# Feature products of a hybrid attention and delta-rule step: eight together in every second step, or four in each

## What is computed

```python
h = _rms(x, w_norm)
proj = h @ w_in                                  # 1024 -> 6152 columns
aq, ak, av, az, bq, bk, bv, bz, bb, ba, ga, gb = jnp.split(proj, ...)
# attention: 4 heads, each a difference of two softmaxes over 64 features
p = softmax(mask(q k^T / 8));  p = p[:, :, 0] - lam * p[:, :, 1];  o_a = rms(p @ v) * silu(az)
# delta rule: short convolution of bq, bk, bv, then chunks with a 128 x 128 state a head
s = s * gl + kg^T (u - w s);  o_b = rms(qg s + qk v_new) * silu(bz)
y = sigmoid(ga) * (o_a @ w_up_a) + sigmoid(gb) * (o_b @ w_up_b);  out = x + y @ w_out
```

## Time and profile before

| | |
|---|---|
| three runs | 1506.8, 1513.76, 1515.07 us (median 1513.76) |
| profiled execution | 1516.26 us |
| its span, first to last instruction | 1514.5 us |
| mean granted clock of TensorE | 0.946 |
| PE busy | 1332.6 us (88%) |
| DVE, ACT, POOL busy | 695.8, 277.7, 453.5 us |
| joint stretch | about 231 to 1237 us |

### The profile page before, as it was taken

How to read it: one execution, slowest core, us unless ns; L and a number is a source line. 1 busy time by engine, 2 the same in 40 slices (tenths; PEclk the granted TensorE clock), 3 DMA queues, 4 the chain that set the end, 5 groups by cost and what they waited for, 6 DMA issues and landing times.

```text
span 1514.5 us, 20691 instructions
## 1 busy us (share of the span) xinstructions
PE 1332.6 (88%) x7189; PEld 684.1 (45%) x7189; DVE 695.8 (46%) x1151; ACT 277.7 (18%) x556; POOL 453.5 (30%) x358
## 2 busy tenths in 40 slices
PE   3999999996997996998887888489999978999999
PEld 3444344453453443444444444145555533554443
DVE  4446205658576665775545454834442204343001
ACT  3112103323222322331111211011211110111000
POOL 0122203425333333443555554346461000000000
PEclk9899999998999997998999999689999999889999
DMA  8120407564655566375798789468786264253121
GB/s 259 27 93 29 148 0 242 176 207 138 205 174 190 167 194 194 118 225 177 215 308 293 246 290 342 160 182 283 281 299 225 78 215 144 84 189 117 55 84 57
DMA packets 167181, 269.25 MB, mean 178 GB/s; under 512 B 29618, under 2 KB 66297, under 8 KB 165916
## 3 DMA queue, kind: packets, MB, share of 16 engines
q1 hardware_dynamic: 107636, 149.64, 31.0%
q10 hardware_dynamic: 59440, 118.28, 23.3%
HBM read 221.63 MB, written 46.40 MB: 177 GB/s over the span
## 4 chain that ended last, share of the span: by engine, by line
PE 69%; DVE 12%; ACTq 4%; issue 4%; DMA 4%; ACT 4%; SPq 2%; POOL 0%; DVEq 0%; POOLq 0%
PE ps L1627 24%; PE ps L1574 11%; PE ps L1940 7%; PE ps L1917 5%; PE ps L1677 4%; PE ps L1650 3%; ACTq L875 2%; ACTq L878 2%; PE ps L1716 2%; DVE sc L1206 1%; SPq L602 1%; DMA work<-in_cache_v 1%; DVE qkv L1382 1%; PE ps L1745 1%; PE ps L1748 1%
## 5 line engine op out<-in xcount | busy, mean ns | idle before, releaser
L1627 PE MATMUL ps<-hT,wbuf 128*128 128x512 f32 x1152 | 546.1, 620 | 0.0
L1627 PEld LDWEIGHTS ps<-hT,wbuf 128*128 128x128 f32 x1152 | 219.3, 199 | 240.1 <-issue 236.7
L700 POOL TENSOR_TENSOR prod<-work,qB 128x512 f32<-128x512 f32 x128 | 176.1, 1387 | 212.5 <-DVE sc L1206 142.9
L700 POOL TENSOR_TENSOR prod<-kbuf,qB 128x512 f32<-128x512 f32 x128 | 164.1, 1299 | 129.8 <-DVE sc L1206 109.6
L1206 DVE TENSOR_REDUCE sc<-prod 128x8 f32<-128x512 f32 x256 | 167.4, 676 | 4.7 <-POOL prod L700 4.3
L1574 PE MATMUL ps<-wbuf,hT 128*128 128x512 f32 x384 | 167.1, 596 | 0.0
L1574 PEld LDWEIGHTS ps<-wbuf,hT 128*128 128x128 f32 x384 | 72.8, 191 | 91.1 <-issue 91.0
L1940 PE MATMUL ps<-hT,work 128*128 128x512 f32 x256 | 110.3, 592 | 0.0
L1917 PE MATMUL ps<-qkv,wbuf 128*128 128x512 f32 x192 | 90.8, 628 | 16.5 <-issue 12.2
L1677 PE MATMUL ps<-ext 64*128 64x512 f32 (+3 forms) x192 | 68.5, 531 | 8.4 <-ACT work L936 8.4
L1940 PEld LDWEIGHTS ps<-hT,work 128*128 128x128 f32 x256 | 48.5, 190 | 60.7 <-issue 60.7
(11 more groups left out here) (325 smaller groups left out, 1367.7 us busy)
## 6 DMA issues: line engine op xcount, KB each, us to landing
work<-in_cache_v ACTq DMA_DIRECT2D x256, 256.0 KB, 4.0
kbuf<-in_cache_k SPq DMA_DIRECT2D x128, 256.0 KB, 3.4
work<-in_cache_k SPq DMA_DIRECT2D x128, 256.0 KB, 3.7
wbuf<-in_w_main ACTq DMA_DIRECT2D x10, 2048.0 KB, 10.0
gsp<-work SPq DMA_DIRECT2D x24, 512.0 KB, 4.4
feat_dram<-qkv ACTq DMA_DIRECT2D x20, 512.0 KB, 4.3
qkv<-in_x_prompt SPq DMA_DIRECT2D x16, 512.0 KB, 4.8
feat_dram<-fst ACTq DMA_DIRECT2D x32, 256.0 KB, 3.9
```

Source lines behind the costliest of these rows:

```text
L700: nc.gpsimd.tensor_tensor(prod[:, p % 4, :], kslot[u], qB[:, j % 2, :], ALU.mult).then_inc(s["page_mul"], 1)
L1627: ins = nc.tensor.matmul(ps[:, 4 + n % 2, :], wbuf[:, wb, kk, f * P:(f + 1) * P], hT[:, kk, half_ * W:(half_ + 1) * W], start=(kk == 0), s ...
```

## The change

The condition `if k % 2 == 0` now holds the eight products of the tile as well as the wait, and the odd step holds none. `f_ready` is raised by the last of the eight. All that stands at the other steps stays where it was, and the queues of the other engines are the same. Lines behind L1627 carry numbers smaller by one in the changed kernel.

```diff
                         pe.wait_ge(s["f_evac"], j * 8 + n - 1)
                     else:
                         pe.wait_ge(once("gb_evac"), nth("gb_evac"))
-                for kk in range(k % 2 * KD // 2, (k % 2 + 1) * KD // 2):
-                    ins = nc.tensor.matmul(ps[:, 4 + n % 2, :], wbuf[:, wb, kk, f * P:(f + 1) * P], hT[:, kk, half_ * W:(half_ + 1) * W],
-                                           start=(kk == 0), stop=(kk == KD - 1))
-                if k % 2:
+                    for kk in range(KD):
+                        ins = nc.tensor.matmul(ps[:, 4 + n % 2, :], wbuf[:, wb, kk, f * P:(f + 1) * P], hT[:, kk, half_ * W:(half_ + 1) * W],
+                                               start=(kk == 0), stop=(kk == KD - 1))
                     fr.inc(ins)
```

## The result

The changed kernel took 1642.97 us (median of 4 runs, 1637.91 to 1645.57) against 1514.41 us before: a ratio of 1.0855, 95% interval 1.0823 to 1.0887. The forecast was 1571, in a range of 1532 to 1606. Its sign held; its size, +57 us, was less than half of the +128.6 that were measured.

What follows compares the result with a forecast made beforehand. TensorE (PE), busy for 88% of the span, was taken as the bound. Place terms summed to 65 us; 65 - 15 - 5 + 12 = 57 us gave 1571 us, range 1532 to 1606.

Steps and rivals of the forecast that it cites:

- scores: Attention's score products (L1677) and three query transposes: 20 places lose the only block covering the exponentials' answer, +31 us.
- rest of attention: Weight transposes, value products behind a copy, and the step from one head to the next: +15 us, ends 0 and 30.
- head's norm: L1733's wait for the head's norm (29.8 us in 4) gets a doubled block as cover each time: -9 us.
- scan: Eight equal scan rounds each lose the odd-step block over the output norm's answer: 8 times 3.2 = 25 us.
- value pages: Tiles complete half a step earlier, so ACT's value loads are not held up and PE's 4.7 us waits may go: -5.
- DVE less behind: In the long places of attention's scores, a PE that pauses finds DVE less far behind: 15 us taken off.
- half clock: Half of some 15 new PE waits over 2 us bring a stretch at clock 0.50, at half price: +12 us.
- three single places: Score waits at 292.4 (loses 1.3 us) and 670.2 (1.85 us grows by 3.4), and one scan round (about 3.2 us).
- rival (1): In attention, DVE and ACT answer within PE's remaining work, so only the scan pays: +20 us, 1534 us; chance 0.14.
- rival (4): GpSimd, DVE and loads set the end everywhere, so moved blocks fall into lost time: no change, 1514 us; chance 0.05.
- Rival (2): Each new PE wait over 2 us is followed by a low-clock stretch, costing 50 us, not 12: 1609 us; chance 0.11.
- Rival (3): In the joint stretch, long blocks hold PE's clock up and only the scan's 25 us is lost: 1479 us; chance 0.04.

Runs made afterwards that it cites:

- The scan alone: The change in chunks 6 to 8 only, blocks of four elsewhere, against the kernel before: 1560.25 us, ratio 1.0297.
- attention alone: The change in chunks 0 to 4 only, blocks of four from chunk 5 on, against the kernel before: 1591.65 us, ratio 1.0466.

## Why the prediction was wrong, point by point

PE's idle time ahead of each group in the joint stretch, changed kernel minus before, beside the terms of the forecast:

| term | forecast, us | measured, us |
|---|---|---|
| scores | +31 | +25 to +27 |
| rest of attention | +15 | +11 |
| head's norm (L1733, now L1732) | -9 | -3.6 |
| key steps | +3 | +4 |
| scan | +25 | +24.8 |
| value pages | -5 | +15.7 |
| sample sums and first solve products | 0 | -5 |
| DVE less behind | -15 | no trace of it |
| idle time, sum | +45 | +73 |
| half clock | +12 | +53 |
| all | +57 | +126 |

**Right: the place-by-place sum.** The five terms that were worked out place by place come to 65 forecast and some 62 measured; that the sum is so close is in part luck, since single terms were off by up to 6 us and offset each other. The three single places on which they rested came out at 1.34 for 1.3, at 5.30 for 5.25 (1.85 and 3.4), and in the scan round at 0.58 + 2.65 = 3.23 us for 3.2. The scan alone and attention alone, each run by itself, confirm that both pay, so rival (1) is refuted: attention's answers were not covered by something else. So is rival (4).

**Wrong: the clock term, "+12, ends 0 and 50".** This is the step that failed. It took 15 new waits of over 2 us, half of them with a stretch at 0.50, at 1.65 us each. The traces have 11 waits of over 2 us before and 34 after, so 23 new ones; 19 new half-clock stretches; and 53 / 19 = 2.8 us for each. All three factors were too small. The price had been halved from 3.3 on no row: the one stretch that the earlier trace rows show had it, the four rows of scores behind the wait in the earlier trace rows show it too, and the one wait without such a stretch was taken as a reason to halve twice, once for the chance and once for the price. The trace of before could have given the chance: of its 11 waits of over 2 us, 10 have a half-clock stretch that begins during the wait or at most 1.2 us behind it. That the clock, and not the grouping, is what costs, is shown by the kernels with extra products: same order, half-clock time 252.6 to 61.9 and 71.7 us, busy time of the real work down by 80 and 75. And if half of the work done at half clock is taken off, PE's busy time is the same, 832 to 837 us, in all of the kernels with blocks of two, four, six and two, and eight (whichever step has the eight); with single products it is 841. Rival (2) had the price right (50), and missed with 1609 because it stood on the same 45 us of idle time. That the sign held says little for the forecast: its clock term was a quarter of what came.

**Wrong: the deductions of 15 and 5.** With them the idle time came to 45 us, and 73 were measured. "A PE that pauses finds DVE less far behind" was argued from one place, and that very place shows the full 3.45 us. "A tile is complete half a step earlier" was to spare PE's waits for value pages; these rose by 15.7 us. What the trace shows is mostly waits for the loads themselves (9 waits, up to 3.5 us, 12.7 of the 15.7). I read it so: the page products of an even and of the next odd step now follow each other without a feature block between them, while a page's load still takes as long. No run here separates this from other causes, and three speak against it: that wait is 9.7 and 10.7 us with the change in the later or in the first chunks alone, but only 6.7 with all eight products in the odd step, where two steps' page products follow each other as well, and 15.6 with two products per half step and 24.6 with one per quarter step, where feature products do lie between. The cause stays open.

**Wrong: "the idle time of PE grows" with busy time "about as before".** The test named for a hit was itself wrong, since it left the clock out of busy time. The scan's chunk was to be 12 us longer and is 21.4 longer, with PE's busy time in it 8.6 us up at a clock of 0.90, where the earlier trace rows have 1.00.

(One end was added up wrong, without weight for the sum: 72 blocks of 3.4 us are 245 us, not 247.)

**Rival (3), refuted.** Eight products in a row did not hold the clock up: half-clock time doubled. The Trainium skill, Perfetto Trace Analysis, section Matmul Optimizations, asks for matmuls back to back in batches. Here the longer batches left longer gaps elsewhere, and the trace disagrees: 14 stretches at half clock with blocks of four, 33 with blocks of eight, and the fastest arrangements without extra work have blocks of two, in all chunks or in the later ones. Its "back-to-back", read as "without gaps", does agree with the kernels that fill the waits (clock 0.97).

## What to carry to other kernels

Work that depends on nothing is best spread over the places where an engine waits for answers, and how finely is to be tried: 8, 6+2, 4 and 2 products a piece gave 1643, 1560, 1514 and 1495 us here, and 1 gave 1507. Read a wait's price as two parts, the idle time and the slower work behind it. When the terms of idle time have been added up place by place, don't shrink the sum by effects that no row shows. And look up what the trace's clock did at all waits of the length of the new ones, not at two of them.

## What the runs showed of the hardware

In six pairs of kernels that differ only in the extra products or in the change, each us less at the lower level (1.2 GHz) gave back 0.40 to 0.48 us of PE's busy time in real work: 53 for 133.1 (before to changed), 80.5 for 190.7 and 74.7 for 180.9 (extra products in the changed kernel), 31.6 for 71.7 (in the kernel before), 38.0 for 78.5 and 31.2 for 71.7 (in two per half step). It is the work inside that time that counts: two per half step has the 119.5 us of the kernel before, but PE works for 89.6 us of it instead of 73.4, and is busy 9.6 us longer; half of the added work is 8.1.

PE time that is spent on nothing can thus pay: products whose results nobody reads, 70 us of PE's time, made a kernel 11.7 us faster (1495.3 to 1483.6 us; the kernel before, timed beside each, took 1515.5 and 1515.1). That depends on where they stand and how they are counted: 138 in 28 waits, counted from the moment their bank is free, paid, though PE still waited 23 us for the bank; 147 in 18 waits, counted from the length of the wait, cost 12 us (1507.3).
